# A hybrid decoder trunk on one core: mixer-end sums one slot later, one table load left out, the last rescale over four slots, and the log difference on GpSimd

## The reference, cut to what matters

```python
def layer(x, ...):
    h = rmsnorm(x, norm_pre[0])
    x = x + 0.5 * rmsnorm(swiglu(h, gate[0], up[0], down[0]), norm_post[0])
    h = rmsnorm(x, norm_pre[1])
    x = x + rmsnorm(mixer(h), norm_post[1])
    h = rmsnorm(x, norm_pre[2])
    x = x + 0.5 * rmsnorm(swiglu(h, gate[1], up[1], down[1]), norm_post[2])

def mixer(h):
    xl, yl, q, k, v, g, gd = split(h @ w_in)
    xc = causal_conv(xl)                        # width 4
    r, i = sigmoid(xc @ wa + ba), sigmoid(xc @ wx + bx)
    log_a = -8 * r * softplus(-lam)
    a, mult = exp(log_a), sqrt(-expm1(2 * log_a))
    hl = scan(a, mult * i * xc)                 # h[t] = a[t] h[t-1] + ...
    lru_out = rmsnorm(hl * gelu(yl), lru_norm)
    o = gated_linear_attention(q, k, v, gd)     # 4 heads
    gla_out = rmsnorm(o, gla_norm) * silu(g)    # one norm per head
    return concat([lru_out, gla_out]) @ w_out
```

## Time and profile before

| | |
|---|---|
| median of 3 runs | 2229.98 us (2228.61 to 2234.95) |
| the profiled execution | 2228.83 us |
| its span (first to last instruction) | 2227.0 us |
| PE busy | 2188.2 us, 98% of the span |
| DVE busy | 1435.2 us, 64% |
| ACT busy | 1281.5 us, 58% |
| POOL busy | 723.6 us, 32% |
| mean granted TensorE clock | 0.994 of full speed |
| DMA | 350.57 MB, mean 157 GB/s |

### The profile page before, as it was taken

The page is one execution under the profiler, slowest core; times in us unless marked ns, Lnnn a source line. Parts: engine busy times, 40 slices in busy tenths (PEclk is TensorE's granted clock), DMA queues, the critical chain, the costliest instruction groups (busy, mean ns, idle before and its releaser), DMA issues.

```text
span 2227.0 us, 39837 instructions
## 1 busy us (share of the span) xinstructions
PE 2188.2 (98%) x16560; PEld 2160.5 (97%) x16560; DVE 1435.2 (64%) x1855; ACT 1281.5 (58%) x1961; POOL 723.6 (32%) x713
## 2 busy tenths in 40 slices
PE   9999999999999999999999999999999999999997
PEld 8999999999999999999999999999989999999997
DVE  7545857658885567845484458676688757576454
ACT  7534657547785556644564356574577755564433
POOL 4112503426544224511241124143274523242112
PEclk9999999999999999999999999999999999999999
DMA  6555555445444455555555555554454444555553
GB/s 232 163 168 162 166 169 158 133 132 162 152 149 136 128 178 161 170 162 164 168 161 162 170 162 164 168 160 131 127 164 149 142 136 134 182 166 154 165 165 121
DMA packets 102403, 350.57 MB, mean 157 GB/s; under 512 B 11441, under 2 KB 16561, under 8 KB 102225
## 3 DMA queue, kind: packets, MB, share of 16 engines
q1 hardware_dynamic: 100992, 346.76, 50.8%
q10 hardware_dynamic: 1232, 1.27, 0.2%
HBM read 343.12 MB, written 4.87 MB: 156 GB/s over the span
## 4 chain that ended last, share of the span: by engine, by line
PE 89%; DVE 7%; POOL 2%; issue 1%; ACT 1%; DMA 0%; SPq 0%; POOLq 0%; DVEq 0%
PE psD L458 84%; DVE wl L1041 3%; POOL ssum L1466 1%; DVE hl L1102 1%; PE psM L562 1%; PE psM L538 1%; DVE y L1094 0%; DVE x L1098 0%; DVE factor L1086 0%; DVE val L1333 0%; PE psM L644 0%; PE psM L615 0%; PE psM L621 0%; DVE factor L1078 0%; DVE val L1327 0%
## 5 line engine op out<-in xcount | busy, mean ns | idle before, releaser
L458 PE MATMUL psD<-hh,wh 128*128 128x288 f32 x3712 | 1111.2, 299 | 9.8 <-DVE hl L1102 4.4
L458 PE MATMUL psD<-hl,wh 128*128 128x288 f32 x3712 | 1098.1, 296 | 0.0
L458 PE MATMUL psD<-hh,wl 128*128 128x288 f32 x3712 | 1094.8, 295 | 0.0
L1041 DVE TENSOR_TENSOR wl<-raw,wh 128x1024 fp32r<-128x1024 f32 (+1 forms) x656 | 825.5, 1259 | 128.3 <-ACT wh L722 127.3
L722 ACT ACTIVATE wh<-raw 128x1024 fp32r<-128x1024 f32 (+1 forms) x656 | 672.4, 1027 | 101.0 <-DMA raw<-in_w_gu 49.9
L458 PEld LDWEIGHTS psD<-hh,wh 128*128 128x128 f32 x3712 | 699.0, 188 | 17.7 <-DVE hl L1102 5.6
L458 PEld LDWEIGHTS psD<-hh,wl 128*128 128x128 f32 x3712 | 702.0, 189 | 0.0
L458 PEld LDWEIGHTS psD<-hl,wh 128*128 128x128 f32 x3712 | 700.2, 189 | 1.4
L1660 POOL TENSOR_TENSOR hidl<-hid,hidh 128x288 fp32r<-128x288 f32 x176 | 213.4, 1212 | 928.9 <-ACT hidh L992 928.9
L458 PE MATMUL psD<-hidh,wh 128*128 128x288 f32 x1408 | 417.5, 297 | 1.5 <-POOL hidl L1660 1.5
L458 PE MATMUL psD<-hidl,wh 128*128 128x288 f32 x1408 | 415.4, 295 | 0.0
(11 more groups left out here) (208 smaller groups left out, 1543.1 us busy)
## 6 DMA issues: line engine op xcount, KB each, us to landing
raw<-in_w_gu SPq DMA_DIRECT2D x352, 512.0 KB, 3.6
raw<-in_w_d SPq DMA_DIRECT2D x128, 448.0 KB, 3.2
raw<-in_w_in SPq DMA_DIRECT2D x80, 512.0 KB, 3.6
raw<-in_w_d SPq DMA_DIRECT2D x64, 512.0 KB, 3.6
raw<-in_w_out SPq DMA_DIRECT2D x32, 512.0 KB, 3.6
gates<-in_w_ax SPq DMA_DIRECT2D x4, 512.0 KB, 4.4
S<-in_st_gla SPq DMA_DIRECT2D x4, 512.0 KB, 5.0
out_gla_s<-S SPq DMA_DIRECT2D x4, 512.0 KB, 5.5
```

What stands on the lines that cost most here:

```text
L458: mm = e.matmul(out, w[:, kt * P:(kt + 1) * P], t[:, kt, :], start=(kt == 0 and part == 0), stop=(kt == KT - 1 and part == 2))
L1041: e.tensor_tensor(wl[u % RING][:, 0:width], raw[u % RING][:, 0:width], wh[u % RING][:, 0:width].bitcast(F32), ALU.subtract).then_inc(lo_re ...
```

## The change

Four edits, in the five generators named above:

- The ten sum matmuls move on TensorE from slot 32 (`T_SUMS + 1`) to slot 33 (`T_SUMS + 2`). ScalarE's and VectorE's slots for what follows are the same as before.
- ScalarE's request for the table set of logarithm and exponential in slot 33 is left out. The request in slot 32 stays.
- In the boundary at the very end of group 0 (last layer, last FFN) VectorE had done the four rescales and two additions in one slot; now it does one pair in each of four slots. Group 1 keeps them in one slot.
- The difference of the two logarithms moves from VectorE to GpSimd, same slot (4t+6), 16 instructions in all.

```diff
@@ TensorE, attention
-                if slot == T_SUMS + 1:
+                if slot == T_SUMS + 2:
                     sums_free()
                     e.wait_ge(stl_ready, i + 1)
                     e.wait_ge(s_ready, 3 * i + 3)
@@ ScalarE, attention
                 if slot == T_SUMS + 2:
-                    e.preload_act_table_set("natural_log_exp_and_others")
                     ln = steps.mark(e.activation(guess5[g][:, 3:5, :], psM[:, 2:4, 0:T], ACT.Ln, scale=1.0 / DV, bias=epsc[:, :]))
@@ VectorE, boundary
-                    if final:
-                        normed = 2 * (3 * l + st)
-                        for k in range(4):
-                            rescale(g, 2 * k, 2)
-                            if k > 1:
-                                e.wait_ge(y_normed[g], normed + k + 1)
-                                add_pair(g, k)
+                    if not final:
+                        rescale(g, 0, 4)
+                k = slot - start - hop
+                if final and k >= 0:
+                    for k in (range(4) if g else (k,)):
+                        rescale(g, 2 * k, 2)
+                        if k > 1:
+                            e.wait_ge(y_normed[g], 2 * (3 * l + st) + k + 1)
+                            add_pair(g, k)
+                    if k == 3:
                         return
-                    rescale(g, 0, 4)
-                if slot == start + hop + 1:
+                if slot == start + hop + 1 and not final:
                     rescale(g, 4, 4)
@@ VectorE, recurrence
-                t = (slot - 6) // R_PERIOD
-                if slot >= 6 and (slot - 6) % R_PERIOD == 0 and t < LT:
-                    e.wait_ge(logs_ready, LT * i + t + 1)
-                    e.tensor_tensor(l1[g][:, :], l1[g][:, :], l2[g][:, :], ALU.subtract).then_inc(ratio_ready, 1)
@@ GpSimd, recurrence
+                t = (slot - 6) // R_PERIOD
+                if slot >= 6 and (slot - 6) % R_PERIOD == 0 and t < LT:
+                    e.wait_ge(logs_ready, LT * i + t + 1)
+                    e.tensor_tensor(l1[g][:, :], l1[g][:, :], l2[g][:, :], ALU.subtract).then_inc(ratio_ready, 1)
```

## The result

| | before | after |
|---|---|---|
| median over all runs, us | 2230.18 (6 runs, 2228.61 to 2234.95) | 2241.92 (6 runs, 2233.71 to 2243.51) |
| ratio after/before | | 1.0044 [1.0033, 1.0055] |
| the profiled execution, us | 2228.83, span 2227.0 | 2233.71, span 2231.9 |
| its mean granted clock of TensorE | 0.994 | 0.992 |

The change makes the kernel 0.44% slower, 11.7 us. Forecast were 2231.8 us and a range up to 2236.5, so the result lies outside. The six executions of after need a second look, each with its mean granted clock: 2233.71 at 0.992 (the profiled one), 2240.37 at 0.990, and 2241.69, 2242.15, 2243.23 and 2243.51 at 0.988. The profiled one is the fastest and has the highest clock. It explains 4.9 us of the 11.7.

A forecast was written before the change was run, and what follows sets the result against it. TensorE, busy 98% of the span, was taken as the bound, so only its stops matter. Mixers +3.6, last rescale -1.8 and log difference 0 gave +1.8 us on the median 2229.98: 2231.8 us, range 2226.0 to 2236.5.

The forecast's parts named there:

- The stops in front of the sums go, and ScalarE stands for them: Mixer sums: TensorE's four stops of 0.98 us vanish (-3.9 us); ScalarE idles some 2.2 us before its table load.
- Product and copy meet: Behind the sums, GpSimd's gated product and VectorE's weight copy run at once; one waits out the other, delaying VectorE.
- Size of the net loss per mixer: Mixer ends: +0.8 us for each of group 0's two, +1.0 for group 1's; +3.6 in all, bounds +2.0 to +5.0.
- case with VectorE first: Group 0 mixers: the copy ends near 504.3, the product holds the Newton step's second instruction; VectorE 0.5 us late.
- one with GpSimd first: Group 0 mixers: the product holds VectorE's copy until 504.65, so it ends at 505.6; VectorE 1.3 us late.
- Edit 3, -1.8 us: Last boundary of group 0: rescales over four slots remove TensorE's stop for a weight's low part, -1.8 us.
- Edit 4, zero: Recurrences: log difference on GpSimd gains and loses equally, zero; bounds -0.8 to +0.6 for each of group 1's two.
- The sum and its translation to the median: Whole kernel: +3.6 - 1.8 + 0 = +1.8 us, applied to the median 2229.98 us, giving 2231.8 us.
- The rivals: Stops stay saved, 2224.3 us (0.15); table load pays exactly, 2228.2 (0.2); slower, 2237.0 (0.1); last rescale fails, 2233.6 (0.05).
- The slower rival: Group 1's recurrences: VectorE's copy waits out GpSimd's difference and addition, 5.2 us more, 2237.0 us; chance 0.1.
- What the changed profile would show: Signs at the sums, ScalarE's load, `hidl`, the copy or Newton step, `wl` and `xc`; `hidl` stops grow to 1.9 to 2.7 us.

The follow-up runs named there:

- e7: Changed kernel with the second half of GpSimd's gated product made three slots later in group 0, five in group 1: 2234.54 us, 1.0018 of before.
- e3: Kernel before with only the last rescale of group 0 spread over four slots: 2228.23 us, ratio 0.9984.
- e4: Kernel before with only the log difference moved from VectorE to GpSimd: 2229.72 us, ratio 0.9993.
- e8: Kernel before with GpSimd making the last `hidl` of four chunks four times over, lengthening TensorE's stops: 2250.94 us, ratio 1.0089.
- e11: e8 with 25 matmuls, output overwritten, in front of each of the four down units: 2241.23 us, 1.0048 of before.
- e6: Changed kernel with 18 matmuls, result overwritten, filling TensorE's stop before each of four down units: 2237.05 us, 1.0026 of before.
- e12: The changed kernel, unedited, timed and profiled once more: 2241.85 us, 1.0042 of before.
- e9: Changed kernel with group 0's sums in their old slot; group 1's sums, guesses and Newton steps all one slot later: 2229.35 us, 0.9993 of before.
- e1: Kernel before with only the sums one slot later, second table load kept: 2240.93 us, ratio 1.0038.
- e10: Changed kernel with guesses and Newton steps moved one slot later along with the sums, in both groups: 2237.99 us, 1.0038 of before.

## Why the prediction was wrong, step by step

- **The stops in front of the sums go, and ScalarE stands for them:** right. 0.98 us each gone; ScalarE idle 2.16 us, forecast 2.2.
- **Product and copy meet:** right. GpSimd was first in group 0 too, and the copy took 2.35 us. e7 takes the meeting away and the stop with it.
- **Size of the net loss per mixer:** forecast +0.8 in group 0 and +1.0 in group 1, +3.6 in all; measured +1.2 each, +4.8. The value was too low, the bounds (+2.0 to +5.0) held it. I had weighed a case with VectorE first against one with GpSimd first in group 0; 0.02 and 0.03 us decided for the second in group 0's two mixers, and in group 1 GpSimd was 0.13 us ahead both times.
- **Edit 3, -1.8 us:** right, -1.9 in the profile, and e3 alone is 0.16% faster, with an interval (0.07 to 0.25%) that holds 1.8 us.
- **Edit 4, zero:** right: e4's ratio is 0.9993 with an interval that holds 1, and the stops for `xc` grew by 0.4 us together.
- **The sum and its translation to the median: the step that failed.** "Sum. +3.6 - 1.8 + 0" has terms for stops and none for TensorE's granted clock. Each stop was priced at its own length, and the same for both sides of the account: a stop of 1.0 us saved against 2.2 us more on a stop of 0.5. But four stops of 2.6 us let the clock fall and four of 0.5 and 1.0 mostly did not: most executions of after are at 0.988, before is at 0.993. e8 and e11 show that idle stops can cost clock; in after itself filling them (e6) gives back 4.8 us, and where the rest comes from is open. Its size: the stops leave 11.7 - 2.9 = 8.8 us. The twelve executions of after (e12 with them) move by some 2.2 us per 0.001 in the mean clock, so the five thousandths from 0.993 to 0.988 are about 11 us, with 2 us of rounding in the clock: enough for the 8.8.
- **The rivals.** None of them had the mechanism. The slower rival's 2237.0 us was put on the recurrences, where nothing happened. The profile of before held the hint that was not used: a clock of 0.994 says that 27 us already ran at 1.2 GHz, in a kernel whose longest stop was 2.3 us. Of these, 8 us lie behind the last matmul, and 14 of the other 17 begin directly behind stops of 2.1 and 2.3 us. What longer stops would add to this belonged into the sum.
- **What the changed profile would show.** All six signs came true (no wait at L668, ScalarE's 2.2 us, stops of 1.9 to 2.7 us, a stretched copy, no `wl` wait, `xc` within 0.8 us), and the time was still outside the range, since none of the signs looked at the clock.

Open: what decides whether a given stop is followed by a slow stretch. After the same stop the clock stayed in one execution and fell in another; e9 kept 0.994 with two stops of 2.2 us while e7 went to 0.991 with four of 1.6; and the slow stretches in the attention come some time behind any long stop. Nor does the sum of the stops order the kernels: for `hidl`, e1 has 12.1 us at 0.990, e10 10.6 at 0.992, after 10.2 at 0.988. That long idle stops can lower the mean is shown by e8 and e11, a rule for the single stop or for their sum is not. Making `stl` earlier, so that the sums could stay in their slot without a stop, was not tried.

## What to carry to other kernels

Where TensorE is busy 98% of the time, a stop of it isn't priced by its length: a longer one can lower the engine's clock as well: four stops of 3.2 and 3.9 us cost 9.7 us beside their length (e8 against e11), and with four stops grown from 0.5 to 2.7 us came 8.8 us, about half of which went with the stops (e6). So before moving a consumer later to spare a short stop, follow the chain of the engine that waits for it to its own next delivery; if that ends in a longer stop, the short one was the cheaper. When an instruction moves to another slot, read which table loads stand round it afterwards (e9). And read the mean granted clock of every execution, not of the profiled one: one profile of after explained 4.9 us of 11.7.

## What was not expected of the hardware

- The clock fell to 1.2 GHz behind idle stops of 2.6 us, in before even of 2.1 and 2.3 us, in the stretch shown for 3.3 us (13 matmuls for 24), and not in every execution.
- Useless matmuls in the place of an idle stop made the kernel faster: 100 of them, -9.7 us (e8 to e11).
- The same difference of 128x288 took 1246 ns on GpSimd and 602 ns on VectorE. Leaving out 16 of them (9.6 us) moved TensorE nowhere.
- The executions of after lie within 9.8 us and those of e10 within 10.7, those of before within 6.3 (within 7.9 over the 74 of the experiments); with the longest stops, in e8, they lie within 0.6 us again, all at the low clock.
